# A gated trunk layer in split fp32: the projection from y by seven products for a pair of blocks

## The reference

```
h = rmsnorm(x, norm_mix_g)
z = gelu(h @ w_in);  u, v = split(z);  v = rmsnorm(v, v_g)
s = einsum('gts,bnsgc->bntgc', tril(w_s), v per chunk of 128) + b_s
x = x + (u * s) @ w_out                      # y = u * s
x = x + relu(rmsnorm(x, norm_mlp_g) @ w1)**2 @ w2     # w1: 1024 x 4096
return rmsnorm(x, final_g)
```

## Time and profile before

| | us |
|---|---|
| median of 3 runs | 1811.26 (1810.73 to 1812.51) |
| the profiled execution | 1810.33 |
| its span, first to last instruction | 1808.6 |
| TensorE busy | 1796.8 |
| VectorE busy | 1113.2 |
| ScalarE busy | 785.8 |
| GpSimd busy | 407.7 |

### The profile page before, as it was taken

How to read it: one execution, slowest core, us unless ns; L and a number is a source line. 1 busy time by engine, 2 the same in 40 slices (tenths; PEclk the granted TensorE clock), 3 DMA queues, 4 the chain that set the end, 5 groups by cost and what they waited for, 6 DMA issues and landing times.

```text
span 1808.6 us, 20167 instructions
## 1 busy us (share of the span) xinstructions
PE 1796.8 (99%) x8132; PEld 1494.0 (83%) x8132; DVE 1113.2 (62%) x1124; ACT 785.8 (43%) x882; POOL 407.7 (23%) x394
## 2 busy tenths in 40 slices
PE   9999999999999999999999999999999999999998
PEld 8888888888888888888788888888888888888886
DVE  3593483485285755565676566674676666766665
ACT  5553544534533744443643443363433335333332
POOL 2442442442340333310011111200243002000002
PEclk9999999999999999999999999999999999999999
DMA  8667666765755788876967778899977655745552
GB/s 326 255 233 258 244 219 228 253 245 189 270 187 172 282 295 296 288 238 201 342 226 256 243 225 260 278 393 304 306 269 277 236 205 192 274 186 192 204 201 102
DMA packets 134477, 445.40 MB, mean 246 GB/s; under 512 B 8176, under 2 KB 9200, under 8 KB 118640
## 3 DMA queue, kind: packets, MB, share of 16 engines
q1 hardware_dynamic: 105472, 327.97, 51.7%
q0 software_dynamic: 25168, 92.80, 14.3%
q10 hardware_dynamic: 3744, 23.34, 3.3%
HBM read 318.26 MB, written 125.83 MB: 246 GB/s over the span
## 4 chain that ended last, share of the span: by engine, by line
PE 97%; DVE 1%; ACT 1%; DMA 1%; issue 0%; ACTq 0%; DVEq 0%; POOLq 0%; POOL 0%
PE bank L1265 66%; PE bank L1100 28%; PE bank L1146 1%; PE bank L1122 1%; DMA hT_raw<-in_xT 1%; PE bank L1149 0%; DVE Y L1038 0%; ACT x_hi L578 0%; DVE Y L1009 0%; ACT hT_hi L631 0%; DVE w_lo L834 0%; DVE x_lo L851 0%; ACT w_hi L563 0%; PE bank L1132 0%; DVE u_lo L840 0%
## 5 line engine op out<-in xcount | busy, mean ns | idle before, releaser
L1265 PE MATMUL bank<-x_hi,u_hi 128*128 128x512 f32 x896 | 348.9, 389 | 1.8 <-DVE c L1009 1.8
L1265 PE MATMUL bank<-x_hi,u_lo 128*128 128x512 f32 x896 | 348.6, 389 | 0.0
L1265 PE MATMUL bank<-x_lo,u_hi 128*128 128x512 f32 x896 | 348.6, 389 | 0.0
L1265 PE MATMUL bank<-d_hi,a_hi 128*128 128x512 f32 x896 | 348.5, 389 | 0.0
L1265 PE MATMUL bank<-d_lo,a_hi 128*128 128x512 f32 x896 | 348.5, 389 | 0.0
L1265 PE MATMUL bank<-d_hi,a_lo 128*128 128x512 f32 x896 | 348.5, 389 | 0.0
L1009 DVE TENSOR_TENSOR Y<-bank,Y 128x512 f32<-128x512 f32 x208 | 138.0, 686 | 180.2 <-PE bank L1265 180.1
L840 DVE TENSOR_TENSOR u_lo<-u_raw,u_hi 128x1024 fp32r<-128x1024 f32 x112 | 147.7, 1318 | 144.4 <-ACT u_hi L568 143.9
L573 ACT ACTIVATE d_hi<-d_raw 128x2048 fp32r<-128x2048 f32 x56 | 107.5, 1919 | 284.6 <-DMA d_raw<-w2sum 159.8
L834 DVE TENSOR_TENSOR w_lo<-w_raw,w_hi 128x2048 fp32r<-128x2048 f32 x47 | 118.4, 2531 | 167.4 <-ACT w_hi L563 167.3
L1265 PEld LDWEIGHTS bank<-x_hi,u_hi 128*128 128x128 f32 x896 | 168.2, 188 | 37.4 <-DVE u_lo L840 2.5
(11 more groups left out here) (111 smaller groups left out, 2752.1 us busy)
## 6 DMA issues: line engine op xcount, KB each, us to landing
a_raw<-a2s SPq DMA_DIRECT2D x56, 1024.0 KB, 7.8
a2s<-sums SPq DMA_DIRECT2D x32, 1280.0 KB, 8.1
job<-in_mlp_w POOLq DMA_DIRECT2D x32, 1024.0 KB, 8.2
u_raw<-w1sum SPq DMA_DIRECT2D x64, 512.0 KB, 4.6
d_raw<-w2sum SPq DMA_DIRECT2D x32, 1024.0 KB, 4.9
w_raw<-in_a_w_in SPq DMA_DIRECT2D x31, 1024.0 KB, 6.8
u_raw<-in_mlp_w SPq DMA_DIRECT2D x48, 512.0 KB, 5.3
d_raw<-in_mlp_w SPq DMA_DIRECT2D x24, 1024.0 KB, 5.2
```

What stands on the lines that cost most here:

```text
L1265: ins = pe.matmul(bank_of(g, j)[:, :], stationary[x_part][:, k, j * P:(j + 1) * P], moving[y_part][:, k, :], start=i in (0, 1, 3) and k == ...
```

## The change

The blocks are done in pairs. Each block has eight units (v and u) of its own; behind the second block of a pair stand seven steps of 48 matmuls, four banks each, that take the place of the eight units of the projection from y of two blocks. Their operands: four of seven weight operands are sums of quarters of `w_out`, made by GpSimd as four new jobs at the head of the list (`wo_jobs`, `wosum`); the four sums of quarters of y are made by VectorE (`out_sum`). Results are added to x1 by VectorE, seven times four banks for a pair (`add_out`, 56 instructions in all, where `add_attention` has 32). The list of jobs has 44 entries now, in the order 4 of w_out, 8 of w1, 4 of x, 8 of w1, 4 of x, 16 of w2; the blocks do 20 of them as before (four in blocks 0 and 2, six in blocks 1 and 3); the loop over the cycles `u`, `FIRST_PARTS` and what follows them are not touched.

The input rows of blocks 1 to 3 are loaded and squared in block 0. The transposes of x1 come for both blocks of a pair in block 2 (all in its v units, at k = 3), and for blocks 2 and 3 before the w1 steps g = 2, 3, 4, 5. Nearly every buffer has a new place. Lines of no weight for the argument are left out:

```diff
-        jobs = w1_jobs[:15] + s_jobs[0] + w1_jobs[15:] + s_jobs[1] + w2_jobs
+        wo_jobs = [("wo", 0, k) for k in range(KU)]
+        jobs = wo_jobs + w1_jobs[:8] + s_jobs[0] + w1_jobs[8:] + s_jobs[1] + w2_jobs
...
+            def rows(q):
+                sp.dma_start(xin[q][:, :, :], x_v[q]).then_inc(xin_later[q - 1], 16)
...
+            for w in range(SLOTS, FIRST):
+                load_w(w)
+                if w < SLOTS + 2:
+                    rows(w - SLOTS + 2)
+                if w == number(1, 0):
+                    sp.wait_ge(squares, x_squares(1) + TT)
+                    features(1, 0)
+                    features(1, 1)
+                if w == number(2, 0):
+                    sp.wait_ge(o_ready, STEPS - 1)
+                    features(2, 0)
+                    features(2, 1)
+                if w == number(3, 0):
+                    features(3, 0)
+                    features(3, 1)
+                for p in range(PAIRS):
+                    if w == out_step(p, 3):
+                        sp.wait_ge(mix_done, (2 * p + 2) * G)
+                        for h in range(2):
+                            sp.dma_start(x1[h][:, :, :], x_v[2 * p + h]).then_inc(x1_loaded[h], 16)
...
                 next_jobs(2)
                 rstd(v_sq, v_squares(q), v_ms, v_ms_done, v_rstd, v_rstd_done, q)
-                next_jobs(3)
-                if q < BLOCKS - 1:
-                    rstd(x_sq, x_squares(q + 1), x_ms, x_ms_done, x_rstd, x_rstd_done, q + 1)
-                rstd(x1_sq, x1_squares(q), x1_ms, x1_ms_done, x1_rstd, x1_rstd_done, q)
+                if q == 0:
+                    for later in range(1, BLOCKS):
+                        cols = slice(later * TT, (later + 1) * TT)
+                        rstd(x_sq[:, cols], x_squares(later), x_ms[:, cols], x_ms_done, x_rstd[:, cols],
+                             x_rstd_done, later)
+                next_jobs(2)
+                if q % 2:
+                    next_jobs(2)
+                    for h in range(2):
+                        cols = slice(h * TT, (h + 1) * TT)
+                        rstd(x1_sq[:, cols], x1_squares(q - 1 + h), x1_ms[:, cols], x1_ms_done, x1_rstd[:, cols],
+                             x1_rstd_done, q - 1 + h)
...
             def squares_x1(q):
+                p, h = q // 2, q % 2
+                act.wait_ge(x1_attn, out_added(p, 5 + h))
+                act.dma_start(x1s[q], x1[h][:, :, :]).then_inc(x1_stored[h], 16)
                 for t in range(TT):
-                    act.wait_ge(x1_attn, q * 2 * TT + TT + t + 1)
-                    square(x1[:, t, :], x1_sq, t, x1_squares(q) + t)
...
+                if q == 2:
+                    keep_x1T(1, 1)
+                if q == 0:
+                    squares_x(3)
...
+            def out_act(p):
+                q = 2 * p + 1
+                split_o(p, 0)
+                split_w(out_step(p, 0))
                 gelu_u(q, 0)
-                split_w(w + 9)
-                for g in range(4):
-                    split_y(q, g)
+                split_w(out_step(p, 1))
                 gelu_u(q, 1)
-                for g in range(4, G):
-                    split_y(q, g)
-                    if g == 5:
-                        split_w(w + 10)
-                if not last:
+                split_o(p, 1)
+                for i in range(2, STEPS):
+                    split_w(out_step(p, i))
+                    split_o(p, i)
+                if p < PAIRS - 1:
+                    split_w(number(q + 1, 0))
                     split_h(q + 1, range(KU))
-                split_w(w + 11)
-                if not last:
-                    for t in range(TT):
-                        act.wait_ge(xin_loaded[t], 16 * (q + 2))
-                        square(xin[:, t, :], x_sq, t, x_squares(q + 1) + t)
+                    squares_x1(q - 1)
                     split_h(q + 1, range(KU, KD))
-                    split_w(w + 12)
-                    split_w(w + 13)
+                    split_w(number(q + 1, 1))
+                    squares_x1(q)
                 else:
                     split_x(0, 0)
                     split_u(0)
+                    squares_x1(q - 1)
                     split_u(1)
                     split_x(0, 1)
...
-                    if g == 4:
-                        keep_x1T(BLOCKS - 1, 0)
-                    if g == 5:
-                        keep_x1T(BLOCKS - 1, 1)
+                    if 2 <= g < 6:
+                        keep_x1T(BLOCKS - 2 + (g - 2) // 2, g % 2)
                     if i < 6:
                         renew(g)
-                    if g == 1:
+                    if g == 0:
                         squares_x1(BLOCKS - 1)
                 elif c == 0 and i in (0, 2, 3, 6):
...
+            def out_sum(p, i):
+                first, second = uT[2 * p], uT[2 * p + 1]
+                a11, a12 = first[:, 0:KU, :], first[:, KU:KD, :]
+                a21, a22 = second[:, 0:KU, :], second[:, KU:KD, :]
+                s2 = o_raw[p][2][:, :, :]
+                if i == 0:
+                    dve.wait_ge(y_done, (2 * p + 1) * G + KU)
+                    dve.wait_ge(o_ready, p * STEPS + 1)
+                    ins = dve.tensor_tensor(a11, a11, a21, ALU.subtract)
+                elif i == 1:
+                    dve.wait_ge(y_done, (2 * p + 2) * G)
+                    dve.wait_ge(o_sums, 4 * p + 1)
+                    dve.wait_ge(products, done(number(2 * p + 1, 7)))
+                    ins = dve.tensor_tensor(s2, a22, a11, ALU.subtract)
+                elif i == 2:
+                    dve.wait_ge(o_sums, 4 * p + 2)
+                    dve.wait_ge(o_ready, p * STEPS + 2)
+                    ins = dve.tensor_tensor(a12, a12, s2, ALU.subtract)
+                else:
+                    dve.wait_ge(products, done(out_step(p, 0)))
+                    ins = dve.tensor_tensor(o_raw[p][0][:, :, :], a21, a22, ALU.add)
+                ins.then_inc(o_sums, 1)
...
+            def block_dve(q):
                 w = number(q, 0)
                 split_w(w + 2)
-                if q > 0:
-                    norm_rows(x1n, x1, x1_rstd, x1_rstd_done, q - 1, x1n_ready)
-                split_w(w + 3)
-                split_w(w + 4)
-                split_w(w + 5)
+                if q == 2:
+                    norm_x1(0)
+                    norm_x1(1)
...
+                if q % 2:
+                    split_o(q // 2, 0)
+                gates(q, 2)
+                if q % 2 == 0:
+                    split_h(q + 1, range(KD))
                 scale_u(q, 1)
-                split_y(q, 3)
...
+            def out_dve(p):
+                q = 2 * p + 1
+                split_o(p, 1)
+                out_sum(p, 0)
+                gates(q, 6)
+                out_sum(p, 1)
+                split_w(out_step(p, 2))
+                out_sum(p, 2)
+                split_o(p, 2)
+                add_out(p, 0)
+                split_w(out_step(p, 3))
+                out_sum(p, 3)
+                split_o(p, 3)
+                add_out(p, 1)
+                for i in range(4, STEPS):
+                    split_w(out_step(p, i))
+                    split_o(p, i)
+                    add_out(p, i - 2)
+                if p < PAIRS - 1:
+                    split_w(number(q + 1, 0))
                     split_h(q + 1, range(KU))
-                split_w(w + 11)
-                if last:
+                    add_out(p, 5)
+                    split_h(q + 1, range(KU, KD))
+                    split_w(number(q + 1, 1))
+                    add_out(p, 6)
+                else:
+                    add_out(p, 5)
                     split_x(0, 0)
                     split_u(0)
-                dve.wait_ge(x1_loaded, 16 * (q + 1))
-                add_attention(q, 0)
-                if not last:
-                    split_h(q + 1, range(KU, KD))
-                    split_w(w + 12)
-                    split_w(w + 13)
-                else:
+                    add_out(p, 6)
                     split_u(1)
                     split_x(0, 1)
...
+            def x1_transposes(q, half, banks):
+                pe.wait_ge(x1n_ready, q * TT + TT)
+                if half or q % 2:
+                    pe.wait_ge(x1T_copied, q * KD + 4 * half)
+                transposes(x1[q % 2], half, banks, x1T_done)
...
                 def first_v(k):
                     if q == 0:
                         pe.wait_ge(hT_ready, k + 1)
+                    if q % 2 and k == 2:
+                        mix_pair(q - 1, 6)
+                    if q == 2 and k == 3:
+                        x1_transposes(0, 0, bank_set(2, 1))
                 def first_v_end(k):
                     if q == 0:
                         pe.wait_ge(hT_ready, KU + k + 1)
-                    elif k == 2:
-                        pe.wait_ge(x1n_ready, q * TT)
-                        transposes(x1n, 0, bank_set(q, 1), x1T_done)
+                    if q == 2 and k == 3:
```

(23 more changed lines are left out.)

464 lines of the change are left out of this document (253 added, 211 removed).

## The result

| | before | after |
|---|---|---|
| median, us (lowest to highest, 4 runs each) | 1810.99 (1810.31 to 1812.51) | 1869.26 (1866.51 to 1871.69) |
| the profiled execution, us | 1810.33 | 1868.84 |
| its span, us | 1808.6 | 1866.8 |

The ratio is 1.0322 (95% interval 1.031 to 1.0334): the change makes the kernel slower by 58 us. The forecast was 1880, in a range from 1838 to 1906.

The account below looks back on a forecast made before the run. TensorE was taken as the bound, with 8132 matmuls back to back. 1810.3 - 21.8 + 56 + (9 + 4 + 9 + 6.6 + 1) + 5 = 1879.1, or 1880 us on the median; range 1838 to 1906.

Parts of the forecast that it names:

- The products: Projection: 14 steps replace 16 units, 96 matmuls less, -21.8 us.
- The jobs: Stalls at w2's d = 9, 16, 23: +56 us; E: end of d = 6; J: one job's time, 23.5.
- (a): Block 0: position weight copies wait behind squares of block 3's rows, +9 us (4 to 14).
- (b): Blocks 0 to 1 and 2 to 3: VectorE's feature splits delay u's second scaling, +4 us (0 to 7).
- (c): Pair 0 to 1: block 0's norm comes late behind VectorE's weight split, +9 us (6 to 12).
- (d): First w1 steps: transposes before g = 3 and 4 wait for x1 copies, +6.6 us (6 to 9).
- (e): Out steps: VectorE has up to 10.1 of 10.88 us of work, +1 us for both pairs (bound 12).
- (f): TensorE's clock: slower matmuls after (a), (c) and the last stall, +5 us (0 to 8).
- jobs alone: Rival, 1849 us: waits in the blocks are as small as their lower bounds; chance 0.12.
- blocks alone: Rival, 1835 us: GpSimd fast enough for chunks 2 and 3, only 16 us at d = 9 remain; chance 0.06.
- VectorE: Rival, 1895 us: VectorE becomes the bound of the out steps, 15 more; chance 0.12.
- The other side: Rival, 1789 us: products save 21.8 us and GpSimd's sums are in DRAM whenever asked for; chance 0.04.

Follow-up runs that it names:

- all_four: Changed kernel with four GpSimd jobs moved forward, block 3's squares later, x1's first norm earlier, x1 copies ahead of bank copies: 1799.51 us.
- before_nine: Kernel before, with four fewer GpSimd jobs in the w1 cycles so that nine are left for the last call: 1856.25 us.
- one_ahead: Changed kernel with one GpSimd job done ahead of the accumulating DMAs, eight left: 1851.88 us.
- start_order: Changed kernel with the squares of block 3's rows behind the position weight copies and the next gelu: 1865.01 us.
- best: all_four with block 2's squares also behind the gelu, and half the next block's feature splits ahead of the second gates: 1799.25 us.
- norm_order: Changed kernel with VectorE's norm of a pair's first block moved right behind the last addition of the out steps: 1857.6 us.
- copy_order: Changed kernel with ScalarE's copies of x1 ahead of its bank copies in the first w1 steps: 1862.21 us.
- vector_more: all_four with two of VectorE's four sums of y done twice in each pair, 2.28 us each: 1812.09 us.
- final: v_earlier, but the job put behind block 0's scale of v is done in the third w1 cycle instead: 1796.2 us.
- v_earlier: best with block 2's squares a little sooner and one GpSimd job moved from ahead of block 0's scale of v to behind it: 1812.39 us.

## Why the prediction was right, point by point

**The products.** -21.8 was right: with most waits gone (`all_four`) the busy time is within 2.0 of the one worked out, and 1.7 of this is lost at the lower clock behind the 3.3 us wait that it still has.

**The jobs.** Forecast 56 us, measured 43.6: without a stall d = 9 would have begun at 1302.8, one matmul's distance behind the one at 1302.57, so E is 1281.0, and d = 23 would have been due at E + 174.1 = 1455.1; it begins at 1498.7. The mechanism and the three places are as stated, and `before_nine` shows that nine left jobs alone bring the same three waits (38.6 us for 38.8). The term was 12.4 too dear, the largest error of the sum: the first left job was stored at E + 23.4 (30 forecast, bounds 26 and 43), for its load took 10 and not 15 with SyncE's queue silent; the eight others took 22.5 each, (1484.45 - 1304.43) / 8 (23.5 forecast); from store to product it was 14.2 at d = 23 (12.2 forecast). 23.4 + 180.0 + 14.2 = 217.6, less 174.1. `one_ahead` gives the other bound of the first job, some E + 43, with full queues.

The row on which J rested holds two kinds of time. With the engines waiting and the queues silent a job takes 15.6 (1378.32 to 1393.95), four additions at 1.28; in a stretch where VectorE works, additions of 3.2 stand among them. The rule of the Trainium skill (page "SBUF — State Buffer", section "SBUF: two separate sides"), that one of the two engines blocks the other for a whole instruction, is borne out by this: the additions at 1319.69 and 1323.00 took 3.23 each while VectorE was in subtractions with two inputs in SBUF, the second of which took 3.39 (the one at 1314.77 took 2.29); and those in the window from 1380 to 1390, where VectorE did nothing, took 1.28 each. That VectorE is busy is not enough: at 1316.97 and 1318.33, beside its additions of a bank to Y (one input in PSUM), GpSimd's took 1.28 as well.

```profile
1316.98 2.48 DVE L1159 TENSOR_TENSOR Y<-bank,Y 128x512 f32<-128x512 f32 x4
1319.37 2.39 DVE L932 TENSOR_TENSOR d_lo<-d_raw,d_hi 128x2048 fp32r<-128x2048 f32 x1
1321.69 3.39 DVE L943 TENSOR_TENSOR a_lo<-a_raw,a_hi 128x2048 fp32r<-128x2048 f32 x1
```

In two of the eight jobs all four additions were short. The stall of 28 us worked out by this rule was too low, since the long additions do occur in the other six; they are worth 21 us of the eight jobs' 180. Its J of some 20 for short additions only was also not what the rows of before give: their long additions hold 2.6 us a job, and 24.7 - 2.6 = 22.0.

**(a) Block 0**, forecast 9, measured 8.0. The rows of block 3 were there at 56.41 (56.6 forecast), the copies follow four squares at 61.00 (61.5), VectorE's part of the position weights ends at 61.61 + 1.29 = 62.90, and TensorE begins at 63.00 (63.5). The list of waits puts this one down to ScalarE's gelu (`vf`), but TensorE goes on 0.10 us behind VectorE's part of the position weights here, in `start_order` and in `best` alike, so these are what it waited for:

```profile
56.41 1.06 ACT L654 ACTIVATE junk<-xin 128x1024 bf16<-128x1024 f32 x1 [1.55 <-DMA xin<-in_x]
...
61.00 1.06 ACT L796 ACTIVATE wsT<-bank 128x512 fp32r<-128x512 f32 x2
61.61 1.29 DVE L1121 TENSOR_TENSOR wsT<-bank,wsT 128x512 fp32r<-128x512 f32 x2 [4.44 <-ACT wsT L796]
```

`start_order` shows that only 4.8 of it belong to block 3's squares; 3.2 hang on block 2's, which push a weight's split back, and `best` removed them.

**(b) Block starts**, forecast 4, measured 3.1 (1.3 and 1.8). The splits took 5.38 and the scaling 2.47 behind them; `best` removed both waits.

**(c) x1's norm**, forecast 9, measured 8.7, removed by `norm_order`. The forecast said that nothing was missing by then but VectorE's turn, and that is the case.

**(d) First w1 steps**, forecast 6.6, measured 7.4 (4.3 and 3.1), cut to 1.2 by `copy_order`.

**(e) The out steps**, forecast 1, measured nothing: no wait at all there. The rival that had VectorE as the bound was wrong for this change, by little: with 4.6 us more per pair (`vector_more`) the waits are 3.5 per pair, so 1.1 of room was there, as the forecast's count of "about 1 us" had it.

**(f) The clock**, forecast 5, measured some 9.7: a cost that had been read from the wrong rows. The slow matmuls behind the first two stalls of w2 are inside the 43.6 (38.8 of it are waits), as the forecast said of them, and the sum leaves 58.2 + 21.8 - 43.6 - 8.0 - 3.1 - 8.7 - 7.4 + 0.5 = 9.7. The price had been read from the transposes at the start, which run at a granted clock of 1.00 in either window and show nothing of it. (The first 44 of them take from 6.3 to 7.8 us in the thirteen traces, all at 1.00; what sets this is open.) The windows above do: 0.50 behind a wait, and full again a few microseconds on. Behind the wait of block 0 TensorE did 12 matmuls in 5 us where 0.227 us a matmul gives 22: 2.3 lost. Sixteen transposes of x1 took 3.65 behind a wait of 4.3, at the lower level, and 1.94 behind one of 3.1, where the clock had not fallen:

```profile
599.18 3.65 PE L1272 MATMUL bank<-ident,x 128*128 128x128 f32 x16 [4.27 <-ACT x L711]
611.99 1.94 PE L1272 MATMUL bank<-ident,x 128*128 128x128 f32 x16 [3.09 <-ACT x L711]
```

The forecast charged (a), (c) and the last stall, but nothing for (d), and too little for each. By whole runs: `before_nine` has three stalls and 7.0 us more of busy time, 2.3 each; the kernel after has six stretches at the lower level, 12.4 us lost, 2.1 each. The Trainium skill (page "TensorE: Matmul & The Clock Gate", section "What's actually happening") has the array at 1.2 GHz after idling and at 2.4 GHz when busy; the trace agrees, with 0.43 and 0.227 us a matmul.

So the jobs were 12 us too dear and the clock 5 too cheap, (b), (a) and (e) together 3 too dear, and the forecast's sum of 1879 stands 10 above the 1868.8 of the profiled execution. The mechanisms and places were right; that the total is no further off is in part luck, as errors of 15 one way and 5 the other cancel. The rival *jobs alone* (1849) fell with the waits of (c) and (d), *blocks alone* (1835) with those at d = 16 and 23, *VectorE* with (e). *The other side* (1789) is 7 below what the change gives once the orders are mended, 1796.2.

Open: `final` saves 14.4 of the 21.8. Its span has 5.1 in the two waits above and 3.4 of busy time over the 1775.0. The load of the u weight that ScalarE splits at 573.26 was issued at 560.69 and awaited for 12.6 us; in `best` the same load was there within 9.8 (563.69 to 573.46). Why it took longer stays open.

## What to carry to other kernels

Work that an engine does in the background has a due time, and adding to the head of its list moves every later item: count the items left at each point where someone waits for one, not the engine's busy share. GpSimd was busy for 24%, and four jobs at the wrong place of its list cost 47 us; each wait in the blocks came from an instruction that stood in a queue ahead of another that was ready or wanted sooner. A stall of TensorE of 4 us or more cost some 2 us on top of itself in every trace here, for the matmuls behind it ran at half pace for a while, and most of those between 2.3 and 3.8 us did the same. In `vector_more` 7.0 us of short waits went with 12.6 us more of time.

## What the runs showed of the hardware that was not expected

The price of a wait in slow matmuls, 2.1 to 2.3 us on the average, is not a matter of its length alone. In the thirteen traces every wait of 4.2 us or more is followed by a granted clock of 0.50 for some microseconds. Of the 17 between 2.3 and 3.8, 14 are: `vector_more` has it behind waits of 2.37, `best` behind its 3.7 (and the same busy time as `all_four`, 1777.4 for 1777.0, since that has it behind its 3.3). The other three, of 3.09, 3.09 and 3.30, are not. Of those from 0.9 to 2.2, one is (1.65, in `v_earlier`). Windows behind the waits of 2.37 in `vector_more`, 3.72 in `best` and 3.09 in the kernel after:

```profile
233.00:235.00 2.00, 2.00 (x6) 1.54 (x6) 2.00 (x3) 0.00 (x0) 0.72 (x1) 0.50 1.04 372
88.00:90.00 2.00, 2.00 (x11) 2.00 (x11) 1.51 (x4) 2.00 (x3) 1.76 (x6) 0.50 0.00 0
612.00:615.00 3.00, 3.00 (x22) 2.78 (x23) 0.75 (x1) 2.70 (x2) 0.78 (x1) 1.00 0.98 349
```

The time of a transfer issued by GpSimd: the 1 MB load of a job took 10 us (1283.93 to 1294.09) when SyncE's queue stood but the accumulating DMA of 1283.18 had just been issued, 5 in the last job before SyncE resumed (1378.32 to 1383.39), and 21.7 when the queues were full (1285.38 to 1307.13, `one_ahead`).

A job of GpSimd costs VectorE as well: a normalization of 128x1024 took 0.75 us in `norm_order` and 1.00 on the average of the same sixteen in the kernel after. There eight of them stand from 303.38 on beside the four additions of a job and take 9.47 us together, up to 1.78 one, and three of the additions 1.60 to 1.62 for 1.28; the other eight take 5.48 us together, as in `norm_order`.
